# A modulation vector summed by GpSimd, with TensorE's sums over partitions one round behind the strip's load

## The reference

```
o = gated_delta_rule_chunked(q, k, v, g, beta)      # first block, the mixer
k, v = jnp.split(mem_n @ w_kv, 2, axis=-1)          # first block, cross attention
mod = jax.nn.silu(c) @ w_ada[layer] + b_ada[layer]  # second block: 1024 -> 3072
shift, scale, gate = jnp.split(mod[:, None, :], 3, axis=-1)
h = rms_norm(x, norm_g[layer]) * (1.0 + scale) + shift
```

## Time and profile before

| | before |
|---|---|
| median of 3 runs | 2943.52 us (2943.43 to 2948.47) |
| the profiled execution | 2942.34 us, span 2940.5 us |
| mean granted clock of TensorE | 0.973 of full speed |
| TensorE busy | 2795.5 us, 95% of the span |
| VectorE busy | 1656.5 us, 56% |
| ScalarE busy | 666.8 us, 23% |
| GpSimd busy | 921.6 us, 31%, in 510 instructions |

### The profile page before, as it was taken

How to read it: one execution, slowest core, us unless ns; L and a number is a source line. 1 busy time by engine, 2 the same in 40 slices (tenths; PEclk the granted TensorE clock), 3 DMA queues, 4 the chain that set the end, 5 groups by cost and what they waited for, 6 DMA issues and landing times.

```text
span 2940.5 us, 34193 instructions
## 1 busy us (share of the span) xinstructions
PE 2795.5 (95%) x14231; PEld 2360.1 (80%) x14231; DVE 1656.5 (56%) x2160; ACT 666.8 (23%) x1055; POOL 921.6 (31%) x510
## 2 busy tenths in 40 slices
PE   6999999988998999999999998999999999999988
PEld 5787799877777878888778886788888888887867
DVE  4789755664513465444544458714156666568646
ACT  3111222223323320000000023211122222234432
POOL 1422000006730632233322324663232111142254
PEclk8999898889999999999999998999999999999999
DMA  3123233225321431111111123562233322266663
GB/s 139 62 97 115 69 97 101 76 69 193 121 66 58 149 111 43 44 48 53 51 50 43 44 86 115 193 227 96 87 121 123 114 101 94 76 222 238 247 255 130
DMA packets 134270, 325.10 MB, mean 111 GB/s; under 512 B 11724, under 2 KB 49508, under 8 KB 133988
## 3 DMA queue, kind: packets, MB, share of 16 engines
q1 hardware_dynamic: 61632, 165.70, 17.4%
q10 hardware_dynamic: 72484, 157.22, 14.9%
HBM read 245.26 MB, written 77.61 MB: 110 GB/s over the span
## 4 chain that ended last, share of the span: by engine, by line
PE 83%; DVE 10%; ACT 3%; issue 2%; POOL 1%; ACTq 1%; DMA 1%; DVEq 0%; POOLq 0%
PE pp L286 28%; PE pp L268 22%; PE pp L471 8%; PE pp L1931 5%; PE pp L2505 4%; PE pp L1176 2%; PE pp L1406 1%; PE pp L1837 1%; DVE ffn_cb L2111 1%; PE pp L1429 1%; PE pp L1817 1%; DVE hgin_b L2321 1%; PE pp L1433 1%; POOL w_lo L3157 1%; PE pp L1418 1%
## 5 line engine op out<-in xcount | busy, mean ns | idle before, releaser
L3155 POOL CAST w_hi<-w_raw 128x1024 fp32r<-128x1024 f32 x252 | 292.1, 1159 | 1925.6 <-PE pp L286 791.5
L3157 POOL TENSOR_TENSOR w_lo<-w_raw,w_hi 128x1024 fp32r<-128x1024 f32 x252 | 634.1, 2516 | 20.2
L286 PE MATMUL pp<-w_hi,act_hi 128*128 128x512 f32 x1344 | 542.0, 403 | 17.6 <-POOL w_lo L3157 12.3
L286 PE MATMUL pp<-w_hi,act_lo 128*128 128x512 f32 x1344 | 528.3, 393 | 0.0
L286 PE MATMUL pp<-w_lo,act_hi 128*128 128x512 f32 x1344 | 525.9, 391 | 0.0
L286 PEld LDWEIGHTS pp<-w_hi,act_hi 128*128 128x128 f32 x1344 | 253.8, 189 | 73.7 <-POOL w_lo L3157 16.1
L286 PEld LDWEIGHTS pp<-w_hi,act_lo 128*128 128x128 f32 x1344 | 253.4, 189 | 58.0
L286 PEld LDWEIGHTS pp<-w_lo,act_hi 128*128 128x128 f32 x1344 | 254.1, 189 | 50.9
L268 PE MATMUL pp<-act_hi,w_hi 128*128 128x512 f32 (+1 forms) x944 | 290.8, 389 | 0.0
L268 PE MATMUL pp<-act_lo,w_hi 128*128 128x512 f32 (+1 forms) x944 | 290.7, 389 | 0.0
L268 PE MATMUL pp<-act_hi,w_lo 128*128 128x512 f32 (+1 forms) x944 | 290.6, 389 | 0.0
(11 more groups left out here) (392 smaller groups left out, 4093.3 us busy)
## 6 DMA issues: line engine op xcount, KB each, us to landing
w_raw<-in_weights SPq DMA_DIRECT2D x292, 512.0 KB, 3.5
z_s<-hg_st ACTq DMA_DIRECT2D x52, 512.0 KB, 3.0
hg_qkb<-hT_s SPq DMA_DIRECT2D x18, 512.0 KB, 7.0
qkvT_s<-mixin_o ACTq DMA_DIRECT2D x12, 512.0 KB, 2.9
gdn_qkv<-qkvT_s ACTq DMA_DIRECT2D x8, 768.0 KB, 5.4
front_x<-in_x ACTq DMA_DIRECT2D x8, 512.0 KB, 5.9
mix_x<-in_x ACTq DMA_DIRECT2D x8, 512.0 KB, 5.6
x_s<-mix_y ACTq DMA_DIRECT2D x8, 512.0 KB, 3.1
```

What stands on the lines that cost most here:

```text
L286: last = pe.matmul(dst, a[:, k, t * P:(t + 1) * P], columns(w, j, k, 0, n), start=(k == 0 and a is high and w is w_hi), stop=(k == NK - 1 ...
L3155: pool.tensor_copy(hi, raw).then_inc(w_split, 1)
L3157: pool.tensor_tensor(lo, raw, hi.bitcast(F32), ALU.subtract).then_inc(w_ready, 1)
```

## The change

GpSimd takes the modulation strips. For each half strip it multiplies the half by the column of `c` that belongs to each of its four blocks of 128 rows (broadcast over 256 columns), adds two and two of the four products and then the last two; the second half's sum is added to that of the first. That leaves 128 partitions x 256 columns per strip in `ada_sum[j]`. Each of the 7 steps waits for the one before. Behind each multiplication GpSimd releases the half strip for the next load. The buffers lie in the place of `w_hi`, free at that time; so GpSimd starts only when the last gate product has been kept, and it splits the first output quarter only when all 12 strips have been added by VectorE.

TensorE then sums over the partitions with two matmuls per strip (4 instructions), `ada_sum[j]` against a column of ones, at the places where the old products stood, but one round later than the strip's load: rounds 1 to 5 have two of them, rounds 6 and 7 one. The strips themselves are loaded two in each of the rounds 0 to 4, and one in rounds 5 and 6. TensorE waits for `ada_summed`, VectorE for `ada_turned`.

To free semaphores, three others are merged: the transposes of the retention stage count on its TensorE semaphore, and a parameter load of the closing stage on the retention's.

```diff
-ADA_JOBS = (0, 2, 2, 2, 2, 1, 1, 1, 1, 0, 0)
+ADA_JOBS = (0, 2, 2, 2, 2, 2, 1, 1, 0, 0, 0)
...
+                ada_sums = {"at": w_hi_at}
+                self.ada_sum = [place(f"gdn_ada_sum{j}", [P, SC], F32, ada_sums) for j in range(N_ADA)]
+                self.ada_parts = place("gdn_ada_parts", [P, NK // 2, SC], F32, ada_sums)
...
-            ADA = ADA_JOBS
+            ADA = (0, *ADA_JOBS[:-1])
...
+            def sum_ada(self, pool):
+                after(pool, self.src.an, f"gate{self.src.GATES - 1}", 0)
+                tt, n = pool.tensor_tensor, 0
+
+                def step(ins):
+                    nonlocal n
+                    n += 1
+                    ins.then_inc(self.ada_summed, 1)
+                    pool.wait_ge(self.ada_summed, n)
+
+                m = self.ada_parts
+                for j, out in enumerate(self.ada_sum):
+                    strip = FIRST_STRIP[f"ada{j}"]
+                    for half in range(2):
+                        pool.wait_ge(w_loaded[half], (RAW_AT[strip] // 2 + 1) * 16)
+                        pool.wait_ge(w_ready, halves_ready(strip, half))
+                        w = w_raw[:, half * HALF:(half + 1) * HALF].rearrange("p (k n) -> p k n", n=SC)
+                        c = ada_c[:, half * NK // 2:(half + 1) * NK // 2].rearrange("p (k a) -> p k a", a=1).broadcast_to((P, NK // 2, SC))
+                        step(tt(m[:, :, :], w, c, ALU.mult))
+                        pool.sem_inc(w_ready, 1)
+                        step(tt(m[:, 0:2, :], m[:, 0:2, :], m[:, 2:4, :], ALU.add))
+                        if half == 0:
+                            step(tt(out[:, :], m[:, 0, :], m[:, 1, :], ALU.add))
+                        else:
+                            step(tt(m[:, 0, :], m[:, 0, :], m[:, 1, :], ALU.add))
+                            step(tt(out[:, :], out[:, :], m[:, 0, :], ALU.add))
...
                 def ada(j):
-                    strip = FIRST_STRIP[f"ada{j}"]
                     if j:
                         pe.wait_ge(self.ada_kept, j)
                     if prep:
                         after(pe, self.pv, "l3", p)
-                    for half in range(2):
-                        pe.wait_ge(w_loaded[half], (RAW_AT[strip] // 2 + 1) * 16)
+                    pe.wait_ge(self.ada_summed, (j + 1) * self.ADA_STEPS)
                     for m in range(2):
-                        for k in range(NK):
-                            c = k * SC + m * P
-                            last = pe.matmul(bank(self.K_)[:, m:m + 1], w_raw[:, c:c + P], ada_c[:, k:k + 1], start=(k == 0), stop=(k == NK - 1))
-                            if m == 1 and k == NK // 2 - 1:
-                                last.then_inc(w_ready, 1)
-                    last.then_inc(w_ready, 1)
+                        last = pe.matmul(bank(self.K_)[:, m:m + 1], self.ada_sum[j][:, m * P:(m + 1) * P], ones[:, 0:1], start=True, stop=True)
+                    last.then_inc(self.ada_turned, 1)
...
-                        if r >= 0:
-                            pe.wait_ge(self.ada_kept, self.ada_of(r)[0])
+                        if sum(self.ADA[:r + 1]):
+                            pe.wait_ge(self.ada_kept, sum(self.ADA[:r + 1]))
...
                 def ada(j):
-                    dve.wait_ge(w_ready, halves_ready(FIRST_STRIP[f"ada{j}"], 2))
+                    dve.wait_ge(self.ada_turned, j + 1)
...
                 if j == FIRST_STRIP["out"]:
                     delta.move_mem(pool)
+                    delta.sum_ada(pool)
+                    pool.wait_ge(delta.ada_kept, N_ADA)
                     pool.wait_ge(w_ready, halves_ready(j, 0))
```

More of the change, by code:

```diff
@@ L172, in build @@
         w_raw = place("w_raw", [P, STRIP])
+        w_hi_at = top["at"]
         w_hi = [place(f"w_hi{s}", [P, HALF], F32R) for s in range(4)]
@@ L1050, in __init__ @@
                 self.mem_moved, self.mem_kept = sem("gdn_mem_moved"), sem("gdn_mem_kept")
+                ada_sums = {"at": w_hi_at}
+                self.ada_sum = [place(f"gdn_ada_sum{j}", [P, SC], F32, ada_sums) for j in range(N_ADA)]
+                self.ada_parts = place("gdn_ada_parts", [P, NK // 2, SC], F32, ada_sums)
+                assert ada_sums["at"] <= w_hi_at + 4 * 4 * HALF
+                self.ada_summed = sem("gdn_ada_summed")
                 self.ada_stored, self.ada_turned = sem("gdn_ada_stored"), sem("gdn_ada_turned")
@@ L1159, in move_mem @@
                     pool.tensor_copy(part[:, :, T - MEM:T], mem[:, GH * n:GH * n + GH, :]).then_inc(self.mem_moved, 1)
+            def sum_ada(self, pool):
[22 more added lines that the diff above has]
+                            step(tt(out[:, :], out[:, :], m[:, 0, :], ALU.add))
+                assert n == self.ADA_STEPS * N_ADA
+            ADA_STEPS = 7
             def mem_product(self, pe, r, part):
@@ L1363, in act @@
                     if o == NT - 1:
-                        act.wait_ge(self.ada_turned, 1)
+                        act.wait_ge(self.ada_turned, N_ADA + 1)
                         act.activation(self.mr[:, :], bank(self.F_)[0:3 * NK, 0:P], ACT.Copy).then_inc(self.ada_turned, 1)
-                        act.wait_ge(self.ada_turned, 2)
+                        act.wait_ge(self.ada_turned, N_ADA + 2)
                         act.dma_start(mod_s.rearrange("o (c p) -> (o c) p", p=P), self.mr[:, :]).then_inc(self.ada_stored, 16)
@@ L2624, in __init__ @@
             def __init__(self, hg):
-                super().__init__("ret", pe="s o ds", act="hz ga sq n_ln n_y",
+                super().__init__("ret", pe="turn s o ds", act="hz ga sq n_ln n_y",
                                  dve="sc g1 g2 m " + " ".join(f"u{j}" for j in range(HH // 2)) + " ss "
                                      + recip_sqrt_steps("n") + " on ong", start=hg.shared)
-                self.turns, self.rTs = Steps(sem("ret_turn"), "turn", 0), Steps(sem("ret_turned"), "rT", 0)
+                self.rTs = Steps(sem("ret_turned"), "rT", 0)
                 self.weighted = Steps(sem("ret_weighted"), "kz qx", 0)
@@ L2648, in __init__ @@
                 self.v_loaded = [sem(f"ret_v_loaded{s}") for s in range(2)]
-                self.gates, self.m_loaded, self.params = sem("ret_gates"), sem("ret_m_loaded"), sem("ret_params")
+                self.gates, self.m_loaded, self.params = sem("ret_gates"), sem("ret_m_loaded"), sem("gate_params")
                 self.on_stored, self.m_stored = sem("ret_on_stored"), sem("ret_m_stored")
@@ L2685, in turned @@
                 def turned(t):
-                    after(act, self.turns, "turn", t)
+                    after(act, PE, "turn", t)
                     if t:
@@ L2744, in turn @@
                         last = pe.transpose(pp[0][:, j * P:(j + 1) * P], self.rot[:, 2 * j:2 * j + 2, :].rearrange("p h e -> p (h e)"), ident[:, :])
-                    self.turns.done(last, "turn")
+                    PE.done(last, "turn")
                 PE.start(pe)
@@ L2823, in dve @@
                     if not last:
-                        after(dve, self.turns, "turn", t)
+                        after(dve, PE, "turn", t)
                         after(dve, self.weighted, "kz", t)
@@ L2883, in __init__ @@
                 self.x_loaded = [sem(f"close_x_loaded{h}") for h in range(2)]
-                self.gx_loaded = sem("close_gx")
                 self.made = sem("close_made")
@@ L2979, in act @@
                 after(act, V, "m", self.HT - 1)
-                act.dma_start(self.gx[:, :], rows[8]).then_inc(self.gx_loaded, 16)
+                act.dma_start(self.gx[:, :], rows[8]).then_inc(R.params, 16)
                 for t in range(self.HT, NT):
@@ L3095, in dve @@
                     if half == 0:
-                        dve.wait_ge(self.gx_loaded, 16)
+                        dve.wait_ge(self.ret.params, 33 + 16)
                         for t in range(self.HT):
```

## The result

The changed kernel takes 2950.67 us, the median of 20 runs; the kernel before takes 2942.93 us, the median of 20 runs beside them. The ratio is 1.002 with a 95% interval of 1.0011 to 1.0029: slower by 0.2%, some 6 us, where 38 us were forecast. The profiled execution's span is 2951.1 us, of 2952.87 in all.

The account below looks back on a forecast made before the run. Each round was taken as one chain TensorE, ScalarE, VectorE, TensorE, with either engine late in places. Rounds summed to +32.5 us after 27 us removed, clock +6, total +38: 2980 us, range 2956 to 3004, lower end widened to 2948.

Parts of the forecast that it names:

- The rule as the prediction words it: VectorE and GpSimd lock shared SBUF ports for whole instructions; reductions and forms of at most one SBUF input are left out.
- the wait for the sums, costed at nothing: TensorE's new wait at the fourth level for the previous round's sums: the train is over long before, so no cost.
- rival three: Broadcast product far slower than the subtraction, next memory strip late, five rounds pay 5 us or more each: 3008, chance 0.07.
- the signs named ahead: GpSimd busy 110 to 130 us, named VectorE lines at means of 1 us and more, rounds 1 to 4 lasting 47 to 52 us.
- The sign of being wrong: The forecast fails if VectorE's lateness under a train is well below 10 us, or if its waits cover it.
- Where the train lies: Walk through VectorE's instructions behind GpSimd's work in each round: 60 us charged, +32.5 us net over the rounds.
- What is removed: Strips' products leave TensorE in rounds 0 to 7: 27 us gained if GpSimd's work is free.
- The clock: TensorE pauses more at round ends; two rounds get the long 1.2 GHz spell at their start: +6 us, range 0 to 16.
- Rival two: Half of the 60 us, as copies and tiny forms slip into gaps between GpSimd's instructions: about 2949, chance 0.12.
- Rival one: GpSimd costs nothing because its instructions fall into VectorE's waits: -27 us, 2916, chance 0.14.

Follow-up runs that it names:

- experiment 1: Changed kernel, but GpSimd only releases each half strip and does none of the 84 products and additions: 2907.10 us, ratio 0.9877 to the kernel before.
- The fill: Changed kernel with 12 unused TensorE matmuls more behind the second sum of rounds 1 to 5: 2930.50 us, ratio 0.9962 to the kernel before.
- the earlier sums: Changed kernel with both strips' sums of a round at the first place, one VectorE addition for both: 2935.48 us, ratio 0.9977 to the kernel before.
- with both: Changed kernel with both sums at the first place, plus 10 or 16 unused matmuls behind the inversion's last step: 2930.39 and 2923.93 us, ratios 0.9954 and 0.9928.
- experiments 1 and 2: The second: kernel before, strips' products kept on TensorE, plus GpSimd's 84 instructions on scratch data: 2972.79 us, ratio 1.0095. The first has its own line.
- Experiment 3's second kernel: Changed kernel with both sums of a round at the first place and no GpSimd arithmetic, modulation vector left out: 2881.15 us, ratio 0.9789 to the kernel before.

## Why the prediction was right or wrong

**The direction and the mechanism were right, the size was not.** The engines take turns by whole instructions, in most of the lines that the prediction named, and the forms with a PSUM operand keep their length. The rule as the prediction words it leaves out every form of at most one SBUF input; copies and scalar forms have one and are held up (the copies 413 ns instead of 292), as its own walk assumes. The products that follow line 1406 are busy 6.5 us, near the 5 forecast (TensorE and its weight loads, line 1438 alone):

```profile
330.00:660.00 330.00, 6.52 (x48) 6.29 (x48) 0.83 0.28 85
```

Between 330 and 660 us no wait of TensorE is for GpSimd or for a transfer, so the wait for the sums, costed at nothing, was nothing; and the next memory strip was in time, which rival three denied. Of the signs named ahead, GpSimd's busy time came out at 105.6 us, not 110 to 130; the stretched lines have means of 0.41 to 1.37 us, not all of 1 and more, and line 1753 (1723 before) stayed at 0.45; rounds 2 to 4 took 47.3 to 48.3 us, as named, round 1 only 43.7. The sign of being wrong came true: VectorE's lateness under a train was to be "well below 10 us", and the stretching in rounds 1 to 4 is 9.5, 7.0, 7.6 and 7.0 us.

By rounds, in us, with the same round limits as above. "Removed" is what the kernel of experiment 1 gains on the kernel before, "trains" what the kernel after takes more than it:

| round | removed, forecast | removed | trains, forecast | trains | stretching |
|---|---|---|---|---|---|
| 0 | 7.6 | 13.3 | 4.6 | 3.4 | 6.2 |
| 1 | 4.0 | 5.0 | 10.4 | 7.6 | 9.5 |
| 2 | 3.0 | 1.2 | 12.4 | 8.6 | 7.0 |
| 3 | 3.8 | 2.7 | 11.6 | 8.6 | 7.6 |
| 4 | 1.5 | 0.5 | 12.0 | 8.6 | 7.0 |
| 5 | 1.5 | 1.0 | 3.0 | 4.4 | 3.3 |
| 6 and 7 | 6.0 | 7.9 | 5.9 | 3.3 | 3.3 |
| sum | 27.4 | 31.5 | 59.9 | 44.5 | 43.8 |

The forecast of the trains is the prediction's net figure of a round plus its removal. The sum of "removed" is less than the 36 us of the medians, because the profiled execution of experiment 1 was the slowest of its four, 3 us above their median, and because some 2 us fall outside these rounds.

**The step that failed is "Where the train lies": its walk charges 60 us, and the trains cost 43** (experiment 1 against the result). Rounds 1 to 4 make up 13 us of the difference. In round 2 the walk had VectorE 13.3 us late at the mask behind line 1007; up to that mask (442.45 in the kernel after) the stretching is 4.2 us, and 7.0 in the whole round. The timelines show why. The third part of the memory product and GpSimd in round 2 of the kernel after:

```profile
424.44 1.89 PE L1212 MATMUL pp<-gdn_mem,w_raw 128*128 128x256 f32 x8
...
430.82 1.89 POOL L1185 TENSOR_TENSOR gdn_ada_parts<-w_raw,ada_c 128x1024 f32<-128x1024 f32 x1 [28.19 <-PE pp L1212]
432.89 1.27 POOL L1187 TENSOR_TENSOR gdn_ada_parts<-gdn_ada_parts 128x512 f32<-128x512 f32 x1 [0.18 <-POOL gdn_ada_parts L1185]
434.25 0.79 POOL L1189 TENSOR_TENSOR gdn_ada_sum<-gdn_ada_parts 128x256 f32<-128x256 f32 x1
435.11 1.89 POOL L1185 TENSOR_TENSOR gdn_ada_parts<-w_raw,ada_c 128x1024 f32<-128x1024 f32 x1
...
449.11 0.72 POOL L1192 TENSOR_TENSOR gdn_ada_sum<-gdn_ada_sum,gdn_ada_parts 128x256 f32<-128x256 f32 x1
```

And VectorE beside it:

```profile
429.78 1.14 DVE L1747 TENSOR_SCALAR mixin_conv<-mixin_conv,mixin_ln 128x256 f32<-128x256 f32 x4
...
432.54 0.46 DVE L1753 TENSOR_TENSOR gdn_qeT<-gdn_qkv,gdn_egb 128x256 f32<-128x256 f32 x1 [1.62 <-PE pp L1558]
432.92 1.53 DVE L1754 TENSOR_TENSOR gdn_qeT<-gdn_qkv,gdn_egb 128x256 f32<-128x256 f32 x1
434.37 1.11 DVE L1758 SCALAR_TENSOR_TENSOR gdn_L<-pp,gdn_sc,gdn_xm 128x128 f32<-128x128 f32 x4
435.41 1.88 DVE L1669 TENSOR_TENSOR gdn_C<-gdn_L,low_masks 128x256 f32<-128x256 f32 x1
...
441.23 1.11 DVE L1776 TENSOR_TENSOR gdn_s<-gdn_s,gdn_sc 128x4 f32<-128x4 f32 x1
```

Three things differ from the walk. The product lasts 1.9 us, not 2.4: I had taken the subtraction with two full inputs. The product differs from it in operation, output type and the broadcast operand, and no run parts these. The train begins 4.5 us behind the third part, not 3.5, and so behind the four scalar forms: the first product runs from 430.82 to 432.71 while VectorE waits for TensorE anyway, where the walk had three of the four pass behind it, the addition and the last step. And VectorE's instruction is not late by one of GpSimd's each time: 0.08 to 0.18 us lie between two of GpSimd's, some of VectorE's forms find one nearly over, and those that follow in a row get through together. The nine stretched ones of round 2 lose 0.8 us each.

**"What is removed" was too small: 36 us, not 27.** The table puts the difference into round 0, 13.3 us instead of 7.6. The prediction took the products' 8.7 us and the wait that they cause, and no clock. TensorE there, in the kernel before and in experiment 1: the strip's products, then the window from 343 us to the end of the round (columns as in the earlier trace rows):

```profile
355.61 5.03 PE L1406 MATMUL pp<-ada_c,w_raw 128*128 128x1 f32 x32 [1.49 <-DVE gdn_att L1735]
...
343.00:371.60 28.60, 25.59 (x165) 23.73 (x164) 13.99 (x38) 4.73 (x11) 0.00 (x0) 0.88 0.34 103
```

```profile
343.00:361.20 18.20, 16.41 (x108) 14.59 (x107) 13.01 (x34) 4.61 (x12) 0.00 (x0) 1.00 0.42 132
```

With the strips in the round the clock is 0.88 and the 32 instructions take 5.03 us instead of the 3.64 of the earlier trace rows; without them it is 1.00 to the round's end. In rounds 2 to 5 the removal gave less than forecast, 5.3 us instead of 9.8. In round 2 of experiment 1 the path from VectorE's line 1723 to the copy at the round's end (1651) does fall from 17.0 to 12.9 us, but then TensorE pauses 4.4 us for the last addition and has a clock of 0.50 for the first 6 us of the next round, and the round as a whole gains 1.2.

**The clock was named and sized too low.** The prediction has +6 for two rounds. The fill gives back 17 us and the earlier sums 13, not added to one another (with both, 0.9954 and 0.9928). It is no separate term of the measured sum: it lies inside the 36 us, which a warm TensorE would have made larger (experiment 1's clock is 0.87 over rounds 1 to 7), and inside the price of the trains. How the 43 us divide between VectorE's lateness and the clock no run shows.

With the measured sizes the sum is -36 + 43 = +7, against -27 + 60 + 6 = +39 by the prediction's terms. Rival two had the number (2949), by luck: its gain of 27 us is 9 too small, its loss of 30 us 13 too small, and the two errors nearly cancel. Its reason, gaps between the instructions, is one of the three above. Rival one falls with experiments 1 and 2; rival three, a product twice as slow, with the 1924 ns.

What stays open: how much of the stretching would vanish if the sums stood in a stage where VectorE has slack. Experiment 3's second kernel, 62 us under the kernel before and without the vector's sums, bounds what there is to win; no kernel with the work elsewhere was run.

## What to carry to other kernels

Work given to an idle GpSimd is paid by VectorE, instruction by instruction, wherever the two read SBUF together. Begin with the sum of VectorE's stretched instructions, from durations of that very form; then take off what fits into VectorE's waits and add what TensorE's clock loses while it waits for the late VectorE. Here 43 to 45 us of stretching cost 28, 43 and 55 us in three kernels. The walk that made every instruction wait for a whole one of the other engine came out too high. When an engine gets lighter, look first at what it will wait for at the end of the loop: here moving two small matmuls earlier and reading less turned a loss of 0.2% into a gain of 0.7%.

## What the runs showed of the hardware

- A GpSimd product of 128x1024 with a broadcast operand takes 1.92 us on the mean, less than the 2.34 us, at the least, of the subtraction with two full inputs.
- VectorE's forms on 128x4 are held up like large ones: the line 1776 takes 0.80 us on the mean instead of 0.16.
- Between two GpSimd instructions that wait for one another lie 0.08 to 0.18 us.
- GpSimd's memsets leave VectorE's two-input forms alone, 411 to 425 ns over 48 of them, and hold up its copies.
- After a pause of 6.72 us TensorE ran at a granted clock of 0.50 for the next 6 us; with 12 unused matmuls in the pause 4.77 us of it were left, the clock behind it was 0.72, and the whole kernel was 0.58% shorter.
- The same 1426 TensorE instructions were busy 220 us at a clock of 0.87 and 237 us at 0.82.
